# Expert stage of a mixture-of-experts layer: from row tiles of 128 with x stationary to units of up to 320 rows with the weights stationary

## The chip, the cores and the metric

One NeuronCore of one Trainium2 chip runs the whole program. The metric is the device time of one execution in microseconds (us). The engines are TensorE (PE in the rows; PEld is its weight load), VectorE (DVE), ScalarE (ACT), GpSimd (POOL) and SyncE (SP), which issues most DMAs. In rows, an SPq or POOLq is the queue of DMAs that the engine issues.

## What is computed

The reference is one encoder layer on 4096 tokens of 1024 numbers, all float32. First a Fourier mixer and a layer norm, then a mixture of experts and a second layer norm. The expert part, cut to its core:

```python
scores = sigmoid(xt @ w_router)                    # 4096 x 32
# best of 4 groups of 8 experts, then the top 2 experts in that group
gate = gate / gate.sum(-1, keepdims=True)
hb = silu(xb @ w_gate[e]) * (xb @ w_up[e])         # 1024 -> 512
y  = hb @ w_down[e]                                # 512 -> 1024
out = segment_sum(y * gate, token)
x = layer_norm(2 ** 0.25 * x + out, g, b)
```

Every token goes to 2 of 32 experts, 8192 rows in all. The reference's inputs send 243, 248, 228, 257, 289, 307, 203, 209, 278, 289, 220, 242, 258, 266, 246, 235, 249, 265, 273, 272, 298, 202, 199, 308, 251, 239, 206, 278, 281, 245, 257 and 351 rows to experts 0 to 31. Sixteen experts have more than 256 rows; only the last has more than 320. Tiles of 128 rows, at least two per expert, are then 80. Units of up to 320 rows are 33: 16 with more than 256 rows ("wide"), 17 with fewer ("narrow"), the second unit of the last expert among these, with 31 rows.

## The kernel before

The kernel has three parts: the Fourier mixer with router (its code is not touched, apart from the layout of the lists), the expert stage, and the final layer norm. Between the first two, the routing writes for each expert a list of (token, gate) pairs to HBM by scattered DMAs, and VectorE works out a table of tile numbers (`tstart`, lines 1260 to 1267) that all engines load into registers.

Matrix products keep float32 precision with three passes: each operand is split in a high part (a cast to float32r, on ScalarE) and a low part (the rest, a subtraction on VectorE), and `PASSES` takes high x high, high x low, low x high. So each weight goes through 12 pieces of 128x1024 per expert: DMA into a ring `wraw` of `SLOTS` (4) pieces, cast (line 981), subtraction (line 1246). Gate and up weights have two buffers (`wgu`, one per expert parity, 64 KiB per partition each); the down weights `wd` have one.

The expert stage runs `expert_tiles` on every engine: a loop over pairs of experts; each expert has two tiles written out and a loop over further tiles under an `If`. A tile on TensorE (`tile`, from line 864) is: gate, 24 matmuls of 512 columns (line 859), with the x rows stationary and the weights moving; up, 48 matmuls of 256 columns in two halves; two transposes of `hid`, four of the next tile's x, and again two and four (lines 852 and 845), the x rows coming from a gather by token number; down, 24 matmuls of 512 columns (line 889), two banks `psY`. ScalarE does silu (999), the high parts of `hidT` (1004) and x (990), weight casts, and half of the gated output (1012). VectorE does the product (1289), the low parts (1295, 1276), weight subtractions, and the other half of the output (1303). The weight pieces of the next expert are spread over the first two tiles by hand (`EARLY`, `LATE`).

GpSimd moves the rows: an indirect gather of 128 rows into `xrow` (1448) and an indirect scatter that adds `yrow` to `sums` in HBM (1456), each scatter waited for before the row numbers are replaced (1459 to 1461). SyncE loads weight pieces in order (`load_piece`), each when its slot has been freed by VectorE's subtraction, and the lists, one DMA for each expert (550).

Of the kernel before, what the change touches and what calls it, by code (L numbers as in the profile page):

```python
# [15 lines left out]
P = 128  # L16
# [4 lines left out]
CH = D // P  # L21
# [30 lines left out]
def shape_constants():  # L52
# [36 lines left out]
    for t in range(TILES):  # L89
        for m in range(P):  # L90
# [5 lines left out]
    ebase = (np.arange(E) * RANKS)[None, :] * np.ones((P, 1))  # L96
    steps = (np.arange(S // P) * P)[None, :] * np.ones((P, 1))
    parts = [("f1", f1), ("ident", np.eye(P)), ("before", before), ("ones", np.ones((P, P))),
             ("cs", cs), ("alt", alt), ("first", first), ("firstg", firstg),
             ("ebase", ebase), ("steps", steps)]  # L100
# [78 lines left out]
def trunk_kernel(nc, x, w_in, w_out, router_w, router_b, w_gate, w_up, w_down, ln_g, ln_b,  # L179
# [5 lines left out]
    lists = nc.dram_tensor("expert_lists", [P * E * BLOCKS, 2], I32).ap()  # L185
# [3 lines left out]
    with ExitStack() as ctx:  # L189
# [17 lines left out]
        def sem(name):  # L207
# [24 lines left out]
        cmp = at("cmp", 176, D)[0:1, :].rearrange("p (e j) -> p e j", e=E)  # L232
# [3 lines left out]
        wgu = [[at(f"wgu{b}_{n}", kib, 2 * CH * F, F32R).rearrange("p (m c f) -> p m c f", m=2, c=CH)  # L236
                for n, kib in (("hi", lo), ("lo", lo + 32))] for b, lo in enumerate((0, 128))]
        wd = [at(f"wd_{n}", kib, FC * D, F32R).rearrange("p (c f) -> p c f", c=FC)
              for n, kib in (("hi", 64), ("lo", 80))]
        mxT = [at(f"mxT_{n}", kib, D, F32R).rearrange("p (c n) -> p c n", c=CH)  # L240
               for n, kib in (("hi", 96), ("lo", 100))]
        hidT = [at(f"hidT_{n}", kib, F, F32R).rearrange("p (c n) -> p c n", c=FC)
                for n, kib in (("hi", 104), ("lo", 106))]
        xrow = at("xrow", 108, D)
        wraw = at("wraw", 112, SLOTS * D).rearrange("p (s d) -> p s d", s=SLOTS)
        yrow, sgate, hid = at("yrow", 192, D), at("sgate", 196, F), at("hid", 198, F)
# [8 lines left out]
        tstart = keep.take("tstart", E + 1, I32)  # L255
        desti = keep.take("desti", 4, I32)
        payg = keep.take("payg", 8, I32)
        entry_t = keep.take("entries", 2 * 2 * BLOCKS, I32)
        rowg = keep.take("rowg", 4, I32)
        ixg = keep.take("ixg", 1, I32)  # L260
        sx = keep.take("sx", 1, I32)
        sxn = keep.take("sxn", 1, I32)
        eps_c, eps2_c = keep.take("eps_c", 1), keep.take("eps2_c", 1)
        zer = keep.take("zer", E)
        rb = keep.take("rb", E)
        mid = keep.take("mid", CH * NG)
        padl = keep.take("padl", 2 * BLOCKS, I32)
# [28 lines left out]
        first, firstg, ebase, steps = (cview(n) for n in ("first", "firstg", "ebase", "steps"))  # L296
# [4 lines left out]
        entries = entry_t.rearrange("p (b r w) -> p b r w", b=2, w=2)  # L301
# [19 lines left out]
        xrow_s = xrow.rearrange("p (d c) -> p c d", c=CH)  # L321
# [37 lines left out]
        tab_ok = sem("tab_ok")  # L359
        ab_ps, ab_hi, ab_lo, xl_ev = sem("ab_ps"), sem("ab_hi"), sem("ab_lo"), sem("xl_ev")  # L360
        wraw_in = [sem(f"wraw_in{n}") for n in range(SLOTS)]
        whi_ok, wlo_ok = sem("whi_ok"), sem("wlo_ok")
        entries_in = [sem("entries_in0"), sem("entries_in1")]
        xrow_in, y_out, ixg_ok, sx_ok = sem("xrow_in"), sem("y_out"), sem("ixg_ok"), sem("sx_ok")
        g_ps, ua_ps, ub_ps, x0_ps, x1_ps, xh_ev, xlo_ev = (
            sem(n) for n in ("g_ps", "ua_ps", "ub_ps", "x0_ps", "x1_ps", "xh_ev", "xlo_ev"))
        silu_ok, hida_ok, hidb_ok, h0_ps, h1_ps, hh_ev, hl_ev = (
            sem(n) for n in ("silu_ok", "hida_ok", "hidb_ok", "h0_ps", "h1_ps", "hh_ev", "hl_ev"))
        y0_ps, y1_ps, ya_ok, yd_ok = (sem(n) for n in ("y0_ps", "y1_ps", "ya_ok", "yd_ok"))
# [56 lines left out]
        def gu_piece(b, part, j):  # L426

            w = wgu[b][part][:, j // 4]
            return w[:, 2 * (j % 4):2 * (j % 4) + 2, :].rearrange("p c f -> p (c f)")

        def block_of(t, lo):

            return (t - lo).with_bounds(min_val=0, max_val=BLOCKS - 1) if t is not lo else 0

        def gate_of(t, b, lo):

            return entries[:, b, ds(block_of(t, lo), 1), 1].bitcast(F32)

        EARLY, LATE = ((), (4, 5)), ((0, 1, 2, 3), (6, 7))

        def entries_there(eng, e, b, kind):
            if kind == 0:
                eng.wait_ge(entries_in[b], 8 * e + 16 - 8 * b)

        def expert_tiles(eng, tile):


            def expert(i, b, last=False):  # L450
                lo = eng.value_load(tstart[0:1, ds(2 * i + b, 1)], min_val=0, max_val=MAX_TILES)
                hi = eng.value_load(tstart[0:1, ds(2 * i + b + 1, 1)], min_val=2, max_val=MAX_TILES)
                tile(lo, 2 * i + b, b, lo, 0, last)
                tile(lo + 1, 2 * i + b, b, lo, 1, last)
                with eng.If(hi > lo + 2):
                    with eng.Fori(lo + 2, hi) as t:
                        tile(t, 2 * i + b, b, lo, 2, last)

            with eng.Fori(0, E // 2 - 1) as i:
                for b in range(2):  # L460
                    expert(i, b)
            expert(E // 2 - 1, 0)
            expert(E // 2 - 1, 1, last=True)
# [1062 lines left out]
```

## Times and profile before

| | |
|---|---|
| runs | 2432.01, 2433.85, 2435.06 us; median 2433.85 |
| profiled execution, span | 2431.3 us (its own time is not given beside it) |
| TensorE busy | 2224.0 us (91%), 12032 matmuls |
| VectorE, ScalarE, GpSimd busy | 1337.8, 909.3, 606.1 us |
| data moved | 438.13 MB, mean 180 GB/s |
| first gate matmul of the expert stage | 847.54 us |
| last down matmuls of the expert stage | 2293.58 us |

The busy time of an engine is a sum over stages. The expert stage is about 1450 us of the span, so its windows are read apart from the rest. The granted clock is a share of 2.4 GHz: 1.00 is 2.4 GHz, 0.50 is 1.2 GHz. Matmuls are pipelined, so their durations overlap; the time from one start to the next is what they cost.

### The profile page before, as it was taken

Reading aid. Unit: us, or ns where it says so; the run is one execution under the profiler, and the core shown is the slowest. Engines: PE = TensorE matmul, PEld = TensorE weight load, DVE = VectorE, ACT = ScalarE, POOL = GpSimd, SP = SyncE. Lnnn points to the kernel's source line nnn. Section 1 sums busy time; section 2 is a strip of 40 time slices with the busy share of each in tenths; the row PEclk is TensorE's granted clock in tenths of the full one; section 3 lists DMA queues with packets and bytes.
Section 4 is the critical chain, followed back from the end, with each engine's and each line's share of the span. In section 5 each row is a group of like instructions: output and inputs, shape, how many; then the busy total and the mean of one; then the engine's idle time right before and its main releaser. Section 6 shows DMA issues by size and latency. Waiting matters only on the chain.

```text
span 2431.3 us, 36221 instructions
## 1 busy us (share of the span) xinstructions
PE 2224.0 (91%) x12032; PEld 1827.0 (75%) x12033; DVE 1337.8 (55%) x2246; ACT 909.3 (37%) x1335; POOL 606.1 (25%) x672
## 2 busy tenths in 40 slices
PE   8999899999998299999999999999999999999700
PEld 3443778878886288888898898888888988988600
DVE  3221348888878555444544544554445455444298
ACT  2221123223333245434534534534345345443143
POOL 1000035454444412111211111111212111111166
PEclk9999999999999599999999999999999999999955
DMA  5980233333433377665765765865667678656386
GB/s 217 289 281 0 80 143 128 126 127 119 142 123 122 124 232 235 182 183 172 241 184 170 245 180 169 241 198 164 178 177 236 189 223 245 181 173 174 78 297 239
DMA packets 128121, 438.13 MB, mean 180 GB/s; under 512 B 24624, under 2 KB 26672, under 8 KB 123952
## 3 DMA queue, kind: packets, MB, share of 16 engines
q1 hardware_dynamic: 88736, 301.72, 35.5%
q0 software_dynamic: 39344, 135.88, 22.5%
q8 instruction: 24, 0.39, 0.1%
q14 instruction: 17, 0.14, 0.0%
HBM read 326.33 MB, written 112.26 MB: 180 GB/s over the span
## 4 chain that ended last, share of the span: by engine, by line
PE 91%; POOL 3%; issue 3%; DVE 2%; DMA 1%; ACT 0%; SPq 0%; POOLq 0%; DVEq 0%
PE ps L859 37%; PE ps L889 18%; PE ps L746 15%; PE ps L683 5%; PE ps L845 3%; POOL fin_r L1489 3%; PE ps L728 2%; PE ps L702 2%; PE ps L780 2%; PE ps L852 2%; PE ps L637 1%; PE ps L767 1%; PE ps L687 1%; PE ps L646 1%; PE ps L742 0%
## 5 line engine op out<-in xcount | busy, mean ns | idle before, releaser
L1246 DVE TENSOR_TENSOR wgu_lo<-wraw,wgu_hi 128x1024 fp32r<-128x1024 f32 x256 | 299.6, 1221 | 176.0 <-ACT wgu_hi L981 156.5
L859 PE MATMUL ps<-wgu_hi,mxT_hi 128*128 128x256 f32 (+1 forms) x1920 | 338.9, 319 | 1.6 <-DVE mxT_lo L1276 1.6
L859 PE MATMUL ps<-wgu_lo,mxT_hi 128*128 128x256 f32 (+1 forms) x1920 | 337.8, 318 | 0.0
L859 PE MATMUL ps<-wgu_hi,mxT_lo 128*128 128x256 f32 (+1 forms) x1920 | 337.8, 318 | 0.0
L859 PEld LDWEIGHTS ps<-wgu_hi,mxT_hi 128*128 128x128 f32 x1920 | 290.9, 191 | 33.7 <-issue 2.4
L859 PEld LDWEIGHTS ps<-wgu_lo,mxT_hi 128*128 128x128 f32 x1920 | 285.3, 191 | 25.0
L859 PEld LDWEIGHTS ps<-wgu_hi,mxT_lo 128*128 128x128 f32 x1920 | 285.3, 191 | 24.9
L981 ACT CAST wgu_hi<-wraw 128x1024 fp32r<-128x1024 f32 x256 | 253.6, 1062 | 20.3 <-DMA wraw<-expert_w_up 20.3
L1289 DVE TENSOR_TENSOR hid<-sgate,ps 128x256 f32<-128x256 f32 x160 | 67.2, 420 | 337.0 <-PE ps L859 337.0
L1456 POOL DMA_INDIRECT sums<-yrow,sx x81 | 131.4, 1622 | 296.4 <-DVE yrow L1303 270.9
L1004 ACT CAST hidT_hi<-ps 128x256 fp32r<-128x256 f32 x160 | 59.6, 372 | 381.7 <-PE ps L852 381.7
L889 PE MATMUL ps<-wd_hi,hidT_hi 128*128 128x512 f32 x640 | 179.5, 402 | 0.0
L889 PE MATMUL ps<-wd_lo,hidT_hi 128*128 128x512 f32 x640 | 171.9, 390 | 0.0
L889 PE MATMUL ps<-wd_hi,hidT_lo 128*128 128x512 f32 x640 | 171.1, 389 | 0.0
L1246 DVE TENSOR_TENSOR wd_lo<-wraw,wd_hi 128x1024 fp32r<-128x1024 f32 x128 | 148.5, 1221 | 40.8 <-ACT wd_hi L981 40.8
L999 ACT ACTIVATE sgate<-ps 128x512 f32<-128x512 f32 x80 | 47.8, 598 | 312.9 <-PE ps L859 312.7
L981 ACT CAST wd_hi<-wraw 128x1024 fp32r<-128x1024 f32 x128 | 126.5, 1051 | 44.0 <-PE ps L889 31.9
L889 PEld LDWEIGHTS ps<-wd_lo,hidT_hi 128*128 128x128 f32 x640 | 120.2, 188 | 26.6
L889 PEld LDWEIGHTS ps<-wd_hi,hidT_lo 128*128 128x128 f32 x640 | 120.1, 188 | 25.2
L1460 POOL COPY sx<-sxn 128x1 int32<-128x1 int32 x81 | 15.1, 186 | 482.3 <-DMA sums<-yrow,sx 482.3
L928 ACT CAST xt_hi<-ps 128x256 fp32r<-128x256 f32 x128 | 40.4, 379 | 245.7 <-PE ps L728 243.9
L889 PEld LDWEIGHTS ps<-wd_hi,hidT_hi 128*128 128x128 f32 x640 | 114.4, 189 | 19.5
(175 smaller groups left out, 3373.3 us busy)
## 6 DMA issues: line engine op xcount, KB each, us to landing
wraw<-expert_w_gate SPq DMA_DIRECT2D x128, 512.0 KB, 6.5
wraw<-expert_w_up SPq DMA_DIRECT2D x128, 512.0 KB, 4.2
wraw<-expert_w_down SPq DMA_DIRECT2D x128, 512.0 KB, 4.4
xch<-x SPq DMA_DIRECT2D x16, 1024.0 KB, 8.8
first_stage<-ych SPq DMA_DIRECT2D x16, 1024.0 KB, 9.6
yt<-first_stage SPq DMA_DIRECT2D x16, 1024.0 KB
fin_r<-sums SPq DMA_DIRECT2D x32, 512.0 KB, 4.0
out<-fin_r SPq DMA_DIRECT2D x32, 512.0 KB, 2.9
```

Source lines behind the costliest of these rows:

```text
L683: mm = nc.tensor.matmul(dst, foldT[:, m, g, c * P:(c + 1) * P], T[:, m, g, h * HALF:(h + 1) * HALF], start=(g == 0), stop=(m == 1 and g == ...
L702: nc.tensor.matmul(bank[s1_bank(n)], f1, xch[:, b, n % 4 // 2, n % 2 * HALF:(n % 2 + 1) * HALF], start=True, stop=True).then_inc(job_ps, 1)
L746: mm = nc.tensor.matmul(ps[:, cols], xt[l][:, m, c, :], w[r][:, c, cols], start=(n == 0 and c == 0 and not edge_row), stop=(n == 2 and c = ...
L845: mm = nc.tensor.transpose(psX0[:, c * P:(c + 1) * P] if half == 0 else psX1[:, c * P:(c + 1) * P], xrow_s[:, 4 * half + c, :], ident)
L859: mm = nc.tensor.matmul(ps, mxT[l][:, c, :], wgu[b][r][:, m, c, lo:hi], start=(n == 0 and c == 0), stop=(n == 2 and c == CH - 1))
L889: mm = nc.tensor.matmul(psY[:, cols], hidT[l][:, c, :], wd[r][:, c, cols], start=(n == 0 and c == 0), stop=(n == 2 and c == FC - 1))
L981: nc.scalar.copy(dst, wraw[:, j % SLOTS, :]).then_inc(whi_ok, 1)
L1004: nc.scalar.copy(hidT[0][:, 2 * half:2 * half + 2, :].rearrange("p c n -> p (c n)"), psH[half]).then_inc(hh_ev, 1)
L1246: nc.vector.tensor_tensor(lo, wraw[:, j % SLOTS, :], hi.bitcast(F32), ALU.subtract).then_inc(wlo_ok, 1)
L1289: nc.vector.tensor_tensor(hid[:, cols], sgate[:, cols], psU[half], ALU.mult).then_inc(ok, 1)
L1456: pool.indirect_dma_start(acc, bass.IndirectOffsetOnAxis(ap=sx[:, 0:1], axis=0), yrow, None, compute_op=ALU.add).then_inc(y_out, 16)
L1489: nc.gpsimd.tensor_tensor(fin_r[:, b, :], fin_r[:, b, :], lnb2, ALU.add).then_inc(fh_ok, 1)
```

## The change

The expert stage is written anew. In words:

- **Units.** The stage is one loop over units of one expert and up to 320 rows. A unit is three row blocks: two of 128 (`t` = 0, 1) and one of 64, which only wide units use. The table holds for each unit its expert, its row in the list, whether it is wide, and a running count of wide units. VectorE makes it with unit numbers on 128 partitions, TensorE turns it into a row with three matmuls (`psTab`), VectorE takes it to `utab`.
- **Stationary weights.** Gate and up go over four blocks `k` of 128 hidden columns; the weight block is stationary, x (transposed, all rows of the unit, 256 or 320 columns) moves. The result comes out with hidden features on the partitions, so `hid` needs no transposes. `If` and `Else` hold the two widths.
- **Down.** For the two blocks of 128 rows as before, with `hidT` stationary. For the 64 rows of a wide unit, `hidC` holds the high part of the 64 rows in its first 64 columns and the low part in the other 64; 8 matmuls per half with both parts of the weights give all four products, of which the two halves of the partitions are added on ScalarE (`ycross`) and VectorE (`y_c`).
- **Buffers.** One buffer each for gate, up and down weights. `wraw` has 6 slots. x rows, output rows and list entries are held for three blocks.
- **Order.** While the up product runs, the gate weights of the next unit are split; up weights follow during down; the down weights of a unit are split at its own start. GpSimd in unit u: gather for u + 1, two or three scatters, each waited for, then the copy of the row numbers.
- **Lists.** 64 lanes instead of 128; a unit's entries are loaded by four small DMAs.

What the engines do after the up product, in the order of their programs (`split j` is weight piece j of the next unit: 0 to 3 gate, 4 to 7 up):

- TensorE: x turns 0 and 1, down of block 0 half 0, x turn 2, half 1, x turn 3, block 1 half 0, the 64 rows' turn (`turn_xc`, if the next unit is wide), half 1, and for a wide unit `down_c` for both halves.
- ScalarE: x turns 0 and 1, `hidC`, split 4, `y_half` 0, x turn 2, split 5, x turn 3, `y_half` 1, the 64 rows' turn, splits 6 and 7, and `y_cross` twice if wide.
- VectorE: x turns 0 and 1, `hidC`, split 3, x turn 2, split 4, `y_half` 0, split 5, x turn 3, the 64 rows' turn, split 6, `y_half` 1, split 7, and `y_c` twice if wide. Before, in its first part: splits 8 to 11 of the unit itself, then splits 0 to 2 of the next, each ahead of one block's product and low part.

The core of the diff:

```diff
-        wgu = [[at(f"wgu{b}_{n}", kib, 2 * CH * F, F32R).rearrange("p (m c f) -> p m c f", m=2, c=CH)
-                for n, kib in (("hi", lo), ("lo", lo + 32))] for b, lo in enumerate((0, 128))]
+        wu = [chunks(f"wu_{n}", kib, CH) for n, kib in (("hi", 0), ("lo", 16))]
+        wg = [chunks(f"wg_{n}", kib, CH) for n, kib in (("hi", 64), ("lo", 80))]
...
@@ SyncE @@
+            with sp.Fori(1, units) as u:
+                e, row = unit_expert(sp, u), unit_row(sp, u)
                 for j in range(PIECES):
+                    load_piece(u, e, j)
+                    if j == 1:
+
+                        own_wait(sp, ent_ok, u, sp_gate)
+                        load_entries(row)
...
@@ TensorE @@
-            def up_or_gate(ps, b, m, lo, hi):
-                for n, (l, r) in enumerate(PASSES):
-                    for c in range(CH):
-                        mm = nc.tensor.matmul(ps, mxT[l][:, c, :],
-                                              wgu[b][r][:, m, c, lo:hi],
-                                              start=(n == 0 and c == 0), stop=(n == 2 and c == CH - 1))
-                return mm
...
+            def gate_or_up(ps, w, k, n):
+                for i, (l, r) in enumerate(PASSES):
+                    for c in range(CH):
+                        mm = nc.tensor.matmul(ps[k % 2][:, 0:n], w[l][:, c, k * P:(k + 1) * P],
+                                              mxT[r][:, c, 0:n], start=(i == c == 0),
+                                              stop=(i == 2 and c == CH - 1))
+                return mm
+
+            def first_products(u, n):
+                pe.wait_ge(wlo_ok, PIECES * u + 4)
+                for k in range(FC):
+                    if k >= 2:
+                        pe.wait_ge(silu_ok, 4 * u + k - 1)
+                    gate_or_up(psG, wg, k, n).then_inc(g_ps, 1)
+                pe.wait_ge(wlo_ok, PIECES * u + GU_PIECES)
+                for k in range(FC):
+                    if k >= 2:
+                        pe.wait_ge(hid_ok, 4 * u + k - 1)
+                    gate_or_up(psU, wu, k, n).then_inc(u_ps, 1)
...
+            def down_c(u, h):
+                cols = slice(h * HALF, (h + 1) * HALF)
+                for r in range(2):
+                    for c in range(FC):
+                        mm = nc.tensor.matmul(psY[h], hidC[:, c, :], wd[r][:, c, cols],
+                                              start=(r == c == 0), stop=(r == 1 and c == FC - 1))
+                mm.then_inc(yc_ps, 1)
+
+            def unit(u, more):
+                wide = unit_wide(pe, u)
+                pe.wait_ge(xh_ev, 4 * u + 4)
+                pe.wait_ge(xlo_ev, 4 * u + 4)
+                pe.wait_ge(xch_ev, u + 1)
+                pe.wait_ge(xclo_ev, u + 1)
+                with pe.If(wide > 0):
+                    first_products(u, UNIT)
+                with pe.Else():
+                    first_products(u, NARROW)
+                if more:
+                    pe.wait_ge(xrow_in, 32 * u + 64)
+                    turn_x(0)
+                    turn_x(1)
+                pe.wait_ge(wlo_ok, PIECES * u + PIECES)
+                pe.wait_ge(ya_ok, 2 * u + 2)
+                pe.wait_ge(yc_ok, 2 * u + 2)
+                down(u, 0, 0, y0_ps)
+                if more:
+                    pe.wait_ge(xlo_ev, 4 * u + 5)
+                    turn_x(2)
+                pe.wait_ge(yd_ok, 2 * u + 2)
+                down(u, 0, 1, y1_ps)
...
+                pe.wait_ge(ya_ok, 2 * u + 3)
+                down(u, 1, 0, y0_ps)
...
+                pe.wait_ge(yd_ok, 2 * u + 3)
+                down(u, 1, 1, y1_ps)
...
@@ ScalarE @@
+            def unit(u, more):
+                wide = unit_wide(act, u)
+                act.wait_ge(y1_ps, 2 * u + 2)
+                act.wait_ge(yc_ps, 2 * u + 2)
+                for k in range(FC):
+                    split(u, GU_PIECES + k)
+                    act.wait_ge(g_ps, 4 * u + k + 1)
+                    nc.scalar.activation(sgate[:, k, :], psG[k % 2][:, 0:UNIT], ACT.Silu).then_inc(silu_ok, 1)
+                for k in range(FC):
+                    if more:
+                        split(u + 1, k)
+                    act.wait_ge(hid_ok, 4 * u + k + 1)
+                    nc.scalar.copy(hidT[:, 0, k, :], hid[:, k % 2, :]).then_inc(hh_ev, 1)
...
@@ GpSimd @@
+                if more:
+                    pool.wait_ge(x_ps, 4 * u + 4)
+                    pool.wait_ge(xc_ps, u + 1)
+                    gather(u + 1)
+                    gather_c(u + 1)
+                    nc.gpsimd.tensor_copy(ent_next, ent_in).then_inc(ent_ok, 1)
+                for t in range(2):
+                    pool.wait_ge(ya_ok, 2 * u + t + 3)
+                    own_wait(pool, yd_ok, 2 * u + t + 3, pool_gate)
+                    scatter(t, P, y_out)
+                    own_wait(pool, y_out, 32 * u + 16 * t + 16, pool_gate)
```

## Rows read from the trace of the kernel before

**Rows 1.** The page's chain that ended last: by engine, by line.

```profile
PE 91%; POOL 3%; issue 3%; DVE 2%; DMA 1%; ACT 0%; SPq 0%; POOLq 0%; DVEq 0%
PE ps L859 37%; PE ps L889 18%; PE ps L746 15%; PE ps L683 5%; PE ps L845 3%; POOL fin_r L1489 3%; PE ps L728 2%; PE ps L702 2%; PE ps L780 2%; PE ps L852 2%; PE ps L637 1%; PE ps L767 1%; PE ps L687 1%; PE ps L646 1%; PE ps L742 0%
```

**Rows 2.** Windows, the expert stage: length, busy (instructions) by engine, clock, DMA, GB/s.

```profile
844.00:2295.00 1451.00, 1449.03 (x8648) 1291.76 (x8648) 732.21 (x938) 639.24 (x889) 267.46 (x400) 1.00 0.66 193
```

**Rows 3.** Timeline of TensorE, first gate matmuls of tiles 1, 3, 4 and 79.

```profile
867.28 1.98 PE L859 MATMUL ps<-wgu_hi,mxT_hi 128*128 128x512 f32 x8
...
903.40 1.98 PE L859 MATMUL ps<-wgu_hi,mxT_hi 128*128 128x512 f32 x8
...
921.58 2.11 PE L859 MATMUL ps<-wgu_hi,mxT_hi 128*128 128x512 f32 x8
...
2276.42 1.98 PE L859 MATMUL ps<-wgu_hi,mxT_hi 128*128 128x512 f32 x8
```

**Rows 4.** Timeline of TensorE over one tile: start, us, what.

```profile
2131.90 1.98 PE L859 MATMUL ps<-wgu_hi,mxT_hi 128*128 128x512 f32 x8
...
2137.34 1.11 PE L859 MATMUL ps<-wgu_hi,mxT_hi 128*128 128x256 f32 x8
...
2143.10 0.38 PE L852 MATMUL ps<-cst,hid 128*128 128x128 f32 x2
...
2144.41 1.17 PE L889 MATMUL ps<-wd_hi,hidT_hi 128*128 128x512 f32 x4
2145.42 1.08 PE L889 MATMUL ps<-wd_lo,hidT_hi 128*128 128x512 f32 x4
...
2149.96 1.98 PE L859 MATMUL ps<-wgu_hi,mxT_hi 128*128 128x512 f32 x8
```

**Rows 5.** Groups by line and form, 900 to 2200 us: busy, mean ns, idle before.

```profile
L1246 DVE TENSOR_TENSOR wgu_lo<-wraw,wgu_hi 128x1024 fp32r<-128x1024 f32 x232 | 271.4, 1221 | 162.1 <-ACT wgu_hi L981 143.2 <-issue 10.6
L981 ACT CAST wgu_hi<-wraw 128x1024 fp32r<-128x1024 f32 x232 | 229.8, 1062 | 0.0
...
L1276 DVE TENSOR_TENSOR mxT_lo<-ps,mxT_hi 128x512 fp32r<-128x512 f32 x144 | 92.8, 686 | 4.7
...
L1289 DVE TENSOR_TENSOR hid<-sgate,ps 128x256 f32<-128x256 f32 x144 | 60.5, 420 | 290.9 <-PE ps L859 290.9
...
L999 ACT ACTIVATE sgate<-ps 128x512 f32<-128x512 f32 x72 | 43.0, 598 | 276.7 <-PE ps L859 276.5
```

**Rows 6.** Timeline of all engines after the last tile.

```profile
2293.58 1.07 PE L889 MATMUL ps<-wd_hi,hidT_lo 128*128 128x512 f32 x4
2294.93 0.75 DVE L1303 TENSOR_SCALAR yrow<-ps,entries 128x512 f32<-128x512 f32 x1 [3.98 <-PE ps L889]
2296.48 1.58 POOL L1481 DMA_INDIRECT sums<-yrow,sx  x1 [11.49 <-DVE yrow L1303]
2302.58 0.82 SPq L592 DMA_DIRECT2D fin_r<-sums  x2
```

**Rows 7.** Timeline of ScalarE at the start of an expert pair.

```profile
927.17 1.28 ACT L999 ACT_TABLE_LOAD   x1
928.46 0.60 ACT L999 ACTIVATE sgate<-ps 128x512 f32<-128x512 f32 x1
```

**Rows 8.** The scatter's line 1456, 81 of them: issue to landing.

```profile
DMA to landing us min/median/max: 5.9/7.5/10.3
```

**Rows 9.** A gather of 128 rows of 4 KiB, line 1370, 32 of them: issue to landing.

```profile
DMA to landing us min/median/max: 4.2/5.1/5.8
```

**Rows 10.** Timeline of all engines ahead of the first tile.

```profile
822.33 1.21 DVE L1260 TENSOR_TENSOR cmp<-base,cst 1x1024 f32<-1x1024 f32 x1
...
836.47 1.01 POOL L1448 DMA_INDIRECT xrow<-h_rows,ixg  x1 [0.92 <-POOL ixg L1467]
...
843.98 1.94 PE L845 MATMUL ps<-cst,xrow 128*128 128x128 f32 x8 [25.96 <-DMA xrow<-h_rows,ixg]
...
847.54 3.62 PE L859 MATMUL ps<-wgu_hi,mxT_hi 128*128 128x512 f32 x8 [1.61 <-DVE mxT_lo L1276]
```

More of the change, by code:

```diff
@@ L443, in entries_there, with piece @@
[L443 to L463, printed above, removed]
+        def piece(part, j):
+            if j < GU_PIECES:
+                w = (wg, wu)[j // 4][part]
+                return w[:, 2 * (j % 4):2 * (j % 4) + 2, :].rearrange("p c f -> p (c f)")
+            return wd[part][:, j - GU_PIECES, :]
@@ L831, in _ @@
             ranks(GROUPS - 1)
-            pe.sem_inc(x1_ps, 1)
-            pe.sem_inc(y1_ps, 1)
+            pe.wait_ge(utab_made, 1)
+            for k in range(3):
+                mm = nc.tensor.matmul(psTab[:, k * P:(k + 1) * P], ucol[:, k:k + 1], ident,
+                                      start=True, stop=True)
+            mm.then_inc(utab_ps, 1)
+            pe.sem_inc(y1_ps, 2)
+            pe.sem_inc(yc_ps, 2)
             pe.wait_ge(p_ev, GROUPS)
@@ new lines, in down @@
+            def down(u, t, h, done):
+                cols = slice(h * HALF, (h + 1) * HALF)
+                for i, (l, r) in enumerate(PASSES):
+                    for c in range(FC):
+                        if t == h == 0 and i != 1:
+                            pe.wait_ge(hh_ev if i == 0 else hl_ev, 4 * u + c + 1)
+                        mm = nc.tensor.matmul(psY[h], hidT[:, l, c, t * P:(t + 1) * P], wd[r][:, c, cols],
+                                              start=(i == c == 0), stop=(i == 2 and c == FC - 1))
+                mm.then_inc(done, 1)
@@ L901, in _ @@
+            pe.wait_ge(xrow_in, 32)
+            turn_x(0)
+            turn_x(1)
+            for k in (2, 3):
+                pe.wait_ge(xlo_ev, k - 1)
+                turn_x(k)
+            pe.wait_ge(xlo_ev, 3)
+            wide0 = unit_wide(pe, 0)
+            with pe.If(wide0 > 0):
+                pe.wait_ge(xcrow_in, 16)
+                turn_xc()
+            with pe.Else():
+                pe.sem_inc(xc_ps, 1)
+            all_units(pe, unit)
         @block.scalar
@@ L1311, in invert @@
+            for j in range(2, GU_PIECES):
+                split(0, j)
+            for k in range(4):
+                turn_x(0, k)
+            take_xc(0)
+            dve.sem_inc(yd_ok, 2)
+            dve.sem_inc(yc_ok, 2)
+            all_units(dve, unit)
             def invert(t, b):
```

566 lines of the change are left out of this document (318 added, 248 removed).

## Prediction

> **What bounds the kernel now.** I read the chain of waits first. It is TensorE for 91% of the span, and line 859 (gate and up) with line 889 (down) are over half of it [rows 1]. So the first question is whether TensorE ever waits in the expert stage. The row of that stretch says no: 1449.03 us busy in 1451.00, at full clock, DMA engines at 0.66 [rows 2]. Next the period. The first gate matmuls of the second tile and of the last one start at 867.28 and 2276.42, 78 tiles apart, so one tile takes 18.066 us; between them lie all loop ends, register loads and skipped third tiles, and the only visible excess is about 0.1 us in one period (903.40 to 921.58) [rows 3]. The stage is therefore a pure count of TensorE instructions. The other engines matter only if their order makes TensorE wait.
>
> **Prices on TensorE** [rows 4]. 24 gate matmuls of 512 columns take 2131.90 to 2137.34, 226.7 ns each. 48 up matmuls of 256 columns take 2137.34 to 2143.10, 120.0 ns each. The difference is 0.417 ns a column, which is one column per cycle of 2.4 GHz, plus 13 ns whatever the width. Twelve transposes take 1.31 us, 109 ns each. Down: 20 matmuls from 2145.42 to 2149.96, 227 ns each, after about 0.1 us of waiting at its start. Together 5.44 + 5.76 + 1.31 + 5.55 = 18.06.
>
> **The change on TensorE.** Before, 80 tiles: 80 x 18.066 = 1445.3 us. After, 33 units, 16 wide and 17 narrow (the counts stand with the reference; the unit of 31 rows is run as 256).
>
> - Narrow unit: gate and up are 2 x 4 x 24 = 192 matmuls of 256 columns, 23.0 us. Down is 48 of 512, 10.9. Sixteen transposes of x, 1.75. With 0.1 of lag, 35.8 us, against 36.1 for the two tiles it replaces. The hidden transposes go, but gate now pays the fixed 13 ns twice as often.
> - Wide unit: 192 matmuls of 320 columns. The trace has no such width. Below it is bounded by the 256-column price (120 ns), above by the 512-column price (227 ns). Two widths and one per-column price make a line, so I take 120.0 + 64 x 0.417 = 146.7 ns, 28.2 us. Down is 48 + 16 = 64 matmuls, 14.5 us. The 64-row transposes I price like full ones, 24 x 0.109 = 2.6. Sum 45.4 us, against 54.2 for three tiles.
> - Stage: 17 x 35.8 + 16 x 45.4 = 1335.0 us, that is 110.3 less. All of the gain is in the wide units, 16 x 8.8 = 141, plus 5 from the narrow ones, less one additional unit (35.8) for the last expert.
>
> If 320 columns cost what 256 do, 82 us more are saved; if what 512 do, 246 more are spent. The common slope speaks against both; I keep 2 ns either way (6 us).
>
> **Do the others keep up?** Prices [rows 5]: a weight cast 1.06 us on ScalarE, its subtraction 1.22 on VectorE, silu 0.60 and the x subtraction 0.69 for 512 columns, the hidden product 0.42 for 256, and the gated output 0.75 [rows 6]; a 512-column cast out of the banks I take like silu. Scaled by columns, ScalarE has about 21 us a unit and VectorE 23 to 25, in 35.8 or 45.4. Totals fit; what counts is order. Let U be the end of the last up matmul and T the end of the unit (U + 12.8 narrow, U + 17.2 wide).
>
> - After U: product 0.49, high part about 0.43, so the last hidden chunk is ready at U + 1.1. TensorE does eight transposes and three matmuls first, until U + 1.6. Covered.
> - Output banks: down of tile 1 needs the two halves of tile 0 taken by U + 7.3 and U + 10.0. ScalarE: last high part to U + 1.2, two x turns to 2.4, the copy for the 64 rows to 2.8, a weight cast to 3.9, its half 0.69, U + 4.6. VectorE: last low part to 1.7, two x turns to 3.2, its copy to 3.6, a weight to 4.8, the third x turn (ScalarE's part ends at 5.2) to 5.9, a weight to 7.1, its half 0.75, U + 7.9. Covered.
> - Single weight buffers: the last up pieces of the next unit are subtracted by about T + 2.5, wanted at T + 11.5. The down pieces are done by T + 13, wanted after T + 24. Double buffering gave slack that nothing used.
> - Silu of the first gate group must be done before the third group begins, at T + 5.8 (narrow). ScalarE comes free at about T + 0.8 and then has a table load, one cast, a second table load and silu, if the unit loop is given both loads as the pair loop is: T + 0.8 + 1.3 + 1.06 + 1.3 + 0.43 = T + 4.9. The margin is 0.9 us, the thinnest here. It rests on a table load costing 1.28 us and no more: the trace shows load at 927.17 and silu at 928.46 [rows 7]. The Trainium skill (ScalarE: Activation LUTs, What ACT_TABLE_LOAD costs) adds some 1.4 us of drain to each switch of set, 2.66 us in all; by that, silu would end at T + 7.6 and 32 units would wait 1.8 us each, 58 us in sum. The trace disagrees, so the sum above stands.
> - GpSimd is serial: scatter, wait, scatter, wait, then the next gather. A scatter lands in 7.5 us in the median, 10.3 at most [rows 8]; a gather by row numbers in 5.1 [rows 9]. GpSimd starts 0.8 us after the output is written (2295.68 to 2296.48, [rows 6]), so scatter 0 starts at U + 8.7, which is T - 4.1 (narrow) or T - 8.6 (wide). Two scatters of 7.6 to 7.9 with their issue bring the narrow unit to T + 11.5; the wide one has a third and is at T + 14.7. Copies, waits and two gather issues take some 3.6, the landing 5: the next rows are there at T + 20 and T + 23.4. TensorE wants it at the next U: T + 23 or T + 28. Covered, except wide followed by narrow (7 times), where it just about meets. I add nothing.
> - Branches: TensorE now takes four per unit. The pair loop now jumps over six tile bodies for about 0.1 us at most [rows 3]. I take 0; the other end, 4 x 0.1 x 33, is 13 us.
> - DMA: 33 instead of 32 sets of weights in 8% less time, so 0.66 becomes about 0.73 [rows 2]. A narrow unit asks as much per us as a two-tile expert does now, and that runs without a stall.
>
> **Head and tail.** The last routing group ends on VectorE where the unit table's arithmetic begins, 822.33 [rows 10]. The new table has some 16 small steps and three matmuls, about 9 us with the two weight splits now ahead of it; it ends before the first rows can arrive, since the gather goes at 836.47, its rows reach TensorE at 843.98 and gate starts at 847.54 [rows 10]. After: four entry loads instead of one, two gathers, and six weight pieces in the same queue instead of four. I take rows 3 us later; then four turns in two banks instead of two, 2 us, and 1.5 us for the second issue: 6.5 us later in all (3 to 12). At the end TensorE's last matmul is at 2293.58 to 2294.65 and the final load goes out at 2302.58 [rows 6]. Scatter 0 of the last unit lands about 2 us after TensorE ends and holds the second one: 1 us more.
>
> **Sum.** 2431.3 - 110.3 + 6.5 + 1.0 = 2328.5 us of span. The median of the runs is 2.5 us above that span, so 2331, 4.2% less.
>
> **Rivals.**
>
> 1. *Small stalls at unit boundaries.* The silu margin of 0.9 us gives way: with two more table loads in a unit (2.6 us, [rows 7]) by 1.7 us, with a slower loop end by some 0.5; 17 to 56 us in 33 units: 2348 to 2387. For: several slacks under 1 us, worked out from single rows. Against: TensorE has no such stall in 80 tiles. Chance 0.2.
> 2. *Branches run dry.* An If whose narrow arm lies 384 instructions on, and a loop end, meet at each unit's start. If a jump costs 1 to 2 us more than the queued matmuls cover, 33 to 66 us: 2364 to 2397. The rows show 0.1 us for the far jump back. The Trainium skill (Runtime: NRT & Kernel Launch, Instruction fetch mechanics) says that a taken branch out of the two fetched pages stops the engine for a fetch, which speaks against this change; the trace shows no such stop on TensorE, perhaps because 24 long matmuls are queued before it. Chance 0.08.
> 3. *GpSimd becomes the bound: slower or no gain.* If each scatter takes the longest landing of before, 10.3 us, wide units deliver at T + 31.5 and narrow ones at T + 25.5. That is 8.5 us late 7 times (wide, then narrow), 3.5 us 9 times (two wide) and 2.5 us 9 times (two narrow): 114 us, which eats the gain: 2445. It decides from 10 us a scatter; at 9 us it costs about 50. For: scatters now follow each other at once, and compete with weights. Against: the median of 7.5. Chance of slower 0.07.
> 4. *The change does not do what it says:* 320 columns cost more than the line. From 183 ns on, 36 ns over it, the gain is gone (3072 x 0.036 = 110). Chance 0.03, within which 0.02 ends within 0.2% or faster.
>
> **Numbers.** Forecast, no stall beyond a few us: 2318 to 2345, chance 0.58. Rivals 1 and 2: 0.28, both faster. Rival 3: 0.07. Rival 4: 0.03. Faster than 2318 (a shorter head, cheaper 64-row turns): 0.04. The range 2318 to 2385 leaves out that 0.04, the slow ends of 1 and 2 (about 0.06) and 3 and 4. A run tells 0.2%, about 5 us, from no change. Faster 0.90, the same 0.02, slower 0.08.
>
> **What would show it.** 192 gate and up matmuls between two groups of down, starting 120 ns apart (narrow) or 147 (wide). First gate to next first gate 35.8 and 45.4 us. First gate near 854, last matmul near 2189. Silu idle before TensorE, not TensorE before silu; no TensorE wait on the gathered rows. It is wrong if TensorE's chain shows waits on silu, on the rows, or on "issue" at unit starts.

## The result: no gain, TensorE waits for gathered rows

The changed kernel takes 2441.74 us in the median of 20 runs (2429.44 to 2452.31), the kernel before 2435.23 (2432.01 to 2439.32). The ratio is 1.0028, 95% interval [1.0015, 1.004]: slightly slower, where 2331 was forecast. The runs now spread over 23 us instead of 7, and the profiled one is among the fastest: span 2429.4, 101 us above the 2328.5 that the sum gave.

The page of the changed kernel, the chain that ended last, by engine and by line (before: [rows 1]):

```profile
PE 67%; DMA 19%; issue 6%; POOL 4%; DVE 2%; POOLq 1%; ACT 0%; SPq 0%; ACTq 0%; DVEq 0%
PE ps L867 19%; PE ps L749 15%; PE ps L891 12%; DMA sums<-yrow_b,ent_now 6%; DMA sums<-yrow_a,ent_now 6%; DMA xrow_b<-h_rows,ent_in 5%; PE ps L686 5%; POOL fin_r L1655 3%; PE ps L855 3%; DMA sums<-yrow_c,ent_now 3%; PE ps L731 2%; PE ps L705 2%; PE ps L783 2%; PE ps L640 1%; PE ps L899 1%
```

TensorE had 91% of the chain; now it has 67%, and scatters (into `sums`) and gathers (from `h_rows`) have 19%. The expert stage in one window, busy time in the order TensorE, its weight load, VectorE, ScalarE, GpSimd (before: [rows 2]):

```profile
860.00:2290.00 1430.00, 1369.72 (x8812) 1278.87 (x8813) 761.37 (x925) 722.92 (x989) 242.63 (x223) 0.98 0.70 192
```

The engine that was idle for 2 us in 1451 is idle for 60 in 1430. No other engine is near full, and the DMA engines are busy 0.70 of the time. So this looks like no shortage of throughput; something arrives late. TensorE's timeline at the first gate matmuls of unit 5 (320 rows) and unit 10 (256 rows), and the middle of unit 10:

```profile
1068.96 1.33 PE L867 MATMUL ps<-mxT_hi,wg_hi 128*128 128x320 f32 x8
1070.13 1.33 PE L867 MATMUL ps<-mxT_lo,wg_hi 128*128 128x320 f32 x8
...
1291.29 1.21 PE L867 MATMUL ps<-mxT_hi,wg_hi 128*128 128x256 f32 x8
...
1313.82 0.76 PE L867 MATMUL ps<-mxT_hi,wu_lo 128*128 128x256 f32 x5
1320.19 0.48 PE L855 MATMUL ps<-cst,xrow_a 128*128 128x128 f32 x1 [5.61 <-DMA xrow_b<-h_rows,ent_in]
...
1321.82 2.05 PE L891 MATMUL ps<-wd_hi,hidT 128*128 128x512 f32 x4
1323.67 1.91 PE L891 MATMUL ps<-wd_lo,hidT 128*128 128x512 f32 x4
```

Groups of eight 320-column matmuls start 1.17 us apart, 146.7 ns for each matmul, as forecast. Gate and up take 23.03 us in a narrow unit and 28.16 in a wide one (forecast 23.0 and 28.2). Then, between up and down, TensorE stands 5.61 us until the next unit's gathered rows are there, and when it starts again the four down matmuls take about twice the 0.9 us of a full clock. The windows say why (columns as in [rows 2]):

```profile
1310.00:1314.00 4.00, 4.00 (x36) 4.00 (x35) 2.61 (x4) 2.31 (x4) 2.32 (x2) 1.00 0.53 161
1314.00:1318.00 4.00, 0.58 (x5) 0.38 (x4) 0.98 (x2) 0.57 (x2) 0.53 (x1) 1.00 0.92 351
1318.00:1320.00 2.00, 0.00 (x0) 0.00 (x0) 0.00 (x0) 0.00 (x0) 0.00 (x0) 0.81 0.08 31
1320.00:1322.00 2.00, 1.80 (x9) 1.81 (x10) 0.03 (x1) 0.59 (x1) 0.19 (x1) 0.50 0.00 0
...
1324.00:1326.00 2.00, 2.00 (x6) 1.52 (x6) 0.85 (x1) 0.04 (x1) 0.00 (x0) 0.50 0.02 4
1326.00:1328.00 2.00, 2.00 (x12) 1.70 (x11) 0.00 (x0) 1.17 (x3) 0.00 (x0) 0.99 0.78 258
```

The granted clock falls from 1.00 to 0.50 (from 2.4 to 1.2 GHz) while TensorE stands and comes back at 1326. A long wait is paid a second time this way.

Over all 33 units I took from the same timeline the time from up's end to the first turn of x (the wait) and from there to the next gate (the rest). The stage is 95.8 us longer than 17 x 35.8 + 16 x 45.4, made of

- 59 us of waits for gathered rows. All narrow units but the first, the twelfth (number 11) and the last have one, of 2.1 to 5.8 us; of the wide ones only three (0.1, 0.7, 1.9);
- 25 us of slower clock. 21 of them stand behind waits: the rest is 1.4 to 2.8 us too long after each of the ten waits of 2.9 us and more, and 0.2 at most after the shorter ones. The other 4 are gate matmuls at half clock, 2.3 us in unit 0 (the clock is at 0.50 there from 860 to 864) and 1.4 in the last unit, behind 3.1 us of idling;
- 3.3 us once, where the loop is left for the last unit;
- 8 us of TensorE's own work, most of it at the 64-row turns of x and at down of the wide units.

The first gate is 6.2 us later than forecast, and the tail 1.65 us longer than before instead of 1. Against that, the sum took the old stage as 1445.3 us, where its first and last matmuls stand 1447.1 apart. 95.8 + 6.2 + 0.65 - 1.8 is the 101 us.

What GpSimd did around that wait, its timeline:

```profile
1283.59 1.68 POOL L1616 DMA_INDIRECT sums<-yrow_a,ent_now  x1 [9.43 <-DVE yrow_a L1410]
1292.76 1.59 POOL L1616 DMA_INDIRECT sums<-yrow_b,ent_now  x1 [7.49 <-issue]
1299.82 1.79 POOL L1616 DMA_INDIRECT sums<-yrow_c,ent_now  x1 [5.47 <-DMA sums<-yrow_b,ent_now]
1308.22 0.99 POOL L1638 COPY ent_now<-ent_next 128x6 int32<-128x6 int32 x1 [6.61 <-DMA sums<-yrow_c,ent_now]
1311.38 1.78 POOL L1602 DMA_INDIRECT xrow_a<-h_rows,ent_in  x1 [2.16 <-issue]
1313.46 1.07 POOL L1602 DMA_INDIRECT xrow_b<-h_rows,ent_in  x1 [0.30 <-issue]
1320.31 0.19 POOL L1626 COPY ent_next<-ent_in 128x6 int32<-128x6 int32 x1 [5.78 <-DMA xrow_b<-h_rows,ent_in]
```

Wide unit 9 ends at T = 1291.29. The forecast had the last scatter done at T + 14.7, the gather issued by T + 18.3 and the rows there at T + 23.4. It was T + 16.9, T + 22.2 and T + 28.9. Every part of the chain is some 1 to 2 us later than priced: the first scatter 0.9, the three together 1.3, from there to the second gather 1.6, the landing 1.6. No part is far off, but the sum had no margin.

### The profile page after: what moved, and what is told of

Read it like the earlier page. It is cut to its first block, busy times and chain, and to the rows that moved or that the text cites. A ratio compares the mean times of both kernels' runs of the same rounds, so it can differ in the third digit from the quotient of the medians.

```text
span 2429.4 us, 37501 instructions
## 1 busy us (share of the span) xinstructions
PE 2152.7 (89%) x12222; PEld 1819.1 (75%) x12223; DVE 1373.7 (57%) x2253; ACT 1000.2 (41%) x1442; POOL 580.5 (24%) x493
## 4 chain that ended last, share of the span: by engine, by line
PE 67%; DMA 19%; issue 6%; POOL 4%; DVE 2%; POOLq 1%; ACT 0%; SPq 0%; ACTq 0%; DVEq 0%
PE ps L867 19%; PE ps L749 15%; PE ps L891 12%; DMA sums<-yrow_b,ent_now 6%; DMA sums<-yrow_a,ent_now 6%; DMA xrow_b<-h_rows,ent_in 5%; PE ps L686 5%; POOL fin_r L1655 3%; PE ps L855 3%; DMA sums<-yrow_c,ent_now 3%; PE ps L731 2%; PE ps L705 2%; PE ps L783 2%; PE ps L640 1%; PE ps L899 1%
## 5 line engine op out<-in xcount | busy, mean ns | idle before, releaser
L891 PE MATMUL ps<-wd_hi,hidT 128*128 128x512 f32 x1056 | 302.1, 412 | 0.4 <-ACT hidT L1089 0.4
L891 PEld LDWEIGHTS ps<-wd_hi,hidT 128*128 128x128 f32 x1056 | 196.8, 195 | 38.3 <-ACT hidT L1089 0.8
L1349 DVE TENSOR_TENSOR wg_lo<-wraw,wg_hi 128x1024 fp32r<-128x1024 f32 x132 | 161.5, 1225 | 92.6 <-ACT wg_hi L1047 92.6
L1349 DVE TENSOR_TENSOR wu_lo<-wraw,wu_hi 128x1024 fp32r<-128x1024 f32 x132 | 160.7, 1218 | 52.3 <-ACT wu_hi L1047 52.2
L867 PE MATMUL ps<-mxT_hi,wg_hi 128*128 128x256 f32 (+1 forms) x1056 | 164.2, 298 | 12.7 <-issue 12.7
L867 PE MATMUL ps<-mxT_lo,wg_hi 128*128 128x256 f32 (+1 forms) x1056 | 163.1, 297 | 0.0
L867 PE MATMUL ps<-mxT_hi,wg_lo 128*128 128x256 f32 (+1 forms) x1056 | 162.5, 296 | 0.0
L867 PE MATMUL ps<-mxT_hi,wu_lo 128*128 128x256 f32 (+1 forms) x1056 | 161.9, 296 | 0.0
L867 PE MATMUL ps<-mxT_lo,wu_hi 128*128 128x256 f32 (+1 forms) x1056 | 161.8, 296 | 0.0
L867 PE MATMUL ps<-mxT_hi,wu_hi 128*128 128x256 f32 (+1 forms) x1056 | 161.8, 296 | 0.0
```

The source lines that it names most:

```text
L867: mm = nc.tensor.matmul(ps[k % 2][:, 0:n], w[l][:, c, k * P:(k + 1) * P], mxT[r][:, c, 0:n], start=(i == c == 0), stop=(i == 2 and c == CH ...
L891: mm = nc.tensor.matmul(psY[h], hidT[:, l, c, t * P:(t + 1) * P], wd[r][:, c, cols], start=(i == c == 0), stop=(i == 2 and c == FC - 1))
L1349: nc.vector.tensor_tensor(piece(1, j), wraw[:, j % SLOTS, :], piece(0, j).bitcast(F32), ALU.subtract).then_inc(wlo_ok, 1)
```

## The experiments

Each run is compared with runs of the kernel before on the same chip. The ratios are to the kernel before; the changed kernel's is 1.0028.

**The scatters out of the chain.** e1_no_scatter leaves out the three scatters of every unit and the waits for them; the experts' output is not added to the sums. e2_no_third_scatter leaves out only the 64-row one.

```diff
                 for t in range(2):
                     pool.wait_ge(ya_ok, 2 * u + t + 3)
                     own_wait(pool, yd_ok, 2 * u + t + 3, pool_gate)
-                    scatter(t, P, y_out)
-                    own_wait(pool, y_out, 32 * u + 16 * t + 16, pool_gate)
                 with pool.If(wide > 0):
                     own_wait(pool, yc_ok, 2 * u + 4, pool_gate)
-                    scatter(2, LANES, yc_out)
-                    own_wait(pool, yc_out, 16 * wides_to(pool, u), pool_gate)
```

> The changed kernel without its three scatters and their waits, so the experts' output is not added to the sums; all else as it is. Theory G (GpSimd's serial chain of scatters makes the next gather late): TensorE waits for rows no more, units take 35.8 to 37 us (narrow) and 44.6 to 45.9 (wide), no clock drop, stage about 1340 us after a first gate at 860; in all 2330 to 2340, some 100 less than the changed kernel. Rival W (the single weight buffers or the weight loads hold TensorE up): most of the stalls stay, 2400 to 2440, with TensorE waiting at gate or down instead of at the turn of the rows.

> The changed kernel without the scatter of the 64 rows of wide units, so their output is left out. Theory G: after a wide unit the next gather goes some 8 us earlier; the stalls of about 5 us in narrow units that follow a wide one, and their clock drops of 1.5 to 2.7 us, vanish (7 units, 45 to 50 us), the 2 to 3 us of narrow after narrow and the cascade behind it stay: 2385 to 2400. If the 64-row scatter is short and only a small part of the chain (as I had priced it, 3 us): 2420 to 2425.

e1_no_scatter: 2346.84 us, ratio 0.9638 [0.9622, 0.9654], 7 us above theory G's range and far from rival W's. No wait at the turn is left, and the stage exceeds its forecast by 13.3 us instead of 95.8 (2.2 of these are the first gate at half clock). e2_no_third_scatter: 2402.91 us, 0.9864 [0.9847, 0.988], 3 us above theory G's range. Every wait in a narrow unit behind a wide one is gone, while in narrow behind narrow eight of nine remain, 3.2 to 6.6 us, with falls of the clock. So the waits come with the scatters, and the third one accounts for less than half. That could be because GpSimd is held up, or because the scatters take DMA time from the gather; these two runs don't tell.

**The order on GpSimd, all work kept.** e4_gather_ahead keeps every transfer and moves the next unit's gather ahead of the wait for the last scatter and of the copy of the row numbers. Unit 0 is taken out of the loop for it.

```diff
             def unit(u, more):
-                wide = unit_wide(pool, u)
                 if more:
                     pool.wait_ge(x_ps, 4 * u + 4)
                     pool.wait_ge(xc_ps, u + 1)
                     gather(u + 1)
+                if not (isinstance(u, int) and u == 0):
+                    scatters_done(u - 1)
+                    own_wait(pool, ent_ok, u + 1, pool_gate)
+                    nc.gpsimd.tensor_copy(ent_now, ent_next).then_inc(entc_ok, 1)
+                    own_wait(pool, entc_ok, u + 1, pool_gate)
+                if more:
                     gather_c(u + 1)
...
-                if more:
-                    own_wait(pool, ent_ok, u + 2, pool_gate)
-                    nc.gpsimd.tensor_copy(ent_now, ent_next).then_inc(entc_ok, 1)
-                    own_wait(pool, entc_ok, u + 2, pool_gate)
```

> The changed kernel with GpSimd's program reordered: the next unit's gather is issued behind the last scatter, before the wait for it and before the row numbers are copied. Same work, same waits between scatters. Theory G: rows arrive 8 to 9 us earlier in every unit, all stalls at the turn vanish, 2335 to 2350. Rival Q (a gather queued behind a scatter of the same queue lands only after it): gather's landing grows from 6.5 to 12 us or more, rows come no earlier, 2400 to 2440.

2349.79 us, ratio 0.9648 [0.9632, 0.9664]: 92 us less than the changed kernel, with the same transfers. The same unit 10 in GpSimd's timeline (its up ends at 1291.2 here):

```profile
1277.17 1.43 POOL L1616 DMA_INDIRECT sums<-yrow_c,ent_now  x1 [5.69 <-DMA sums<-yrow_b,ent_now]
1278.90 1.67 POOL L1602 DMA_INDIRECT xrow_a<-h_rows,ent_in  x1 [0.30 <-issue]
1280.88 0.97 POOL L1602 DMA_INDIRECT xrow_b<-h_rows,ent_in  x1 [0.30 <-issue]
1285.17 0.89 POOL L1633 COPY ent_now<-ent_next 128x6 int32<-128x6 int32 x1 [3.33 <-DMA sums<-yrow_c,ent_now]
1290.18 0.40 POOL L1637 COPY ent_next<-ent_in 128x6 int32<-128x6 int32 x1 [4.12 <-DMA xrow_b<-h_rows,ent_in]
```

The gather is issued 1.7 us behind the third scatter instead of 11.6, and its rows are there before TensorE asks. Gathers now run beside a scatter and land later (median 7.8 us instead of 6.3), which eats little of that. Rival Q, by which the transfers would only wait for each other in the queue, falls. Behind narrow units the gather now waits for the list entries instead (82 us in 16 waits of GpSimd), which costs TensorE nothing here.

**How much slack there is.** e8_gpsimd_delay and e10_ahead_delay put the same idle work into both orders.

```diff
+                    for k in range(12):
+                        nc.gpsimd.tensor_copy(idle[:, k, :], ent_next)
                     nc.gpsimd.tensor_copy(ent_now, ent_next).then_inc(entc_ok, 1)
```

> The changed kernel with twelve additional small copies (of 6 numbers in each of 128 partitions, into a buffer that nobody reads; 0.19 us each, 2.3 us together) on GpSimd in each unit, behind the wait for the last scatter and ahead of the copy of the row numbers. Theory G (GpSimd's chain of scatters, waits and gather sets the period): nearly every one of the 32 turns moves by 2.3 us, with some further falls of TensorE's clock: 70 to 95 us more, 2510 to 2540. Rival D (the rows are late because the DMA engines are full of weights, whatever GpSimd does): under 2460.

> e4_gather_ahead with the same twelve copies (2.3 us) on GpSimd in each unit, again ahead of the copy of the row numbers, which now stands behind the issue of the next gather. Theory G (that order took GpSimd's chain off the path, with slack left): within 5 us of e4_gather_ahead, 2348 to 2355. Rival S (it is still at the edge): 20 to 70 us more, 2370 to 2420.

e10_ahead_delay: 2349.98 us, 0.9646 [0.9631, 0.9661], no difference from e4_gather_ahead; the new order has the slack. e8_gpsimd_delay: 2459.73 us, 1.0104 [1.0088, 1.0119], 18 us over the changed kernel. That is far under the 70 that theory G asked for at least, and 0.3 us under the rival's bound of 2460, which runs between 2447.86 and 2462.37 can't tell from it. Unit 10 shows it (timeline, GpSimd's rows and then TensorE's):

```profile
1308.51 2.17 POOL L1640 COPY idle<-ent_next 128x6 int32<-128x6 int32 x12 [6.16 <-DMA sums<-yrow_c,ent_now]
...
1314.27 0.98 POOL L1603 DMA_INDIRECT xrow_b<-h_rows,ent_in  x1 [0.30 <-issue]
1320.00 0.19 POOL L1627 COPY ent_next<-ent_in 128x6 int32<-128x6 int32 x1 [4.75 <-DMA xrow_b<-h_rows,ent_in]
...
1319.89 0.48 PE L856 MATMUL ps<-cst,xrow_a 128*128 128x128 f32 x1 [5.50 <-DMA xrow_b<-h_rows,ent_in]
```

The gather is issued 0.8 us later than in the changed kernel (1314.27 against 1313.46), yet its rows come 0.3 us earlier. Over the six narrow units behind a wide one it is issued 0.9 us later on average, and TensorE goes on 0.4 us later. So most of the additional 2.2 us of copies never reaches the gather's issue, and the moment of issue isn't all that sets its landing. From 1314 to 1318 the DMA engines are at 0.92 in the changed kernel; the down pieces of the weights were asked for just before:

```profile
1312.30 13.05 SPq L568 DMA_DIRECT2D wraw<-expert_w_down  x2
```

**The weights.** e9_light_weights loads a quarter of each piece. (A piece is 1024 columns wide, so 256 of 1024 are loaded, not the 128 of 512 that the expectation names.)

```diff
-                sp.dma_start(wraw[:, j % SLOTS:j % SLOTS + 1, :], w[:, ds(e, 1), h, :]
+                n = D if is_first(u) else D // 4
+                sp.dma_start(wraw[:, j % SLOTS:j % SLOTS + 1, 0:n], w[:, ds(e, 1), h, 0:n]
                              ).then_inc(wraw_in[j % SLOTS], 16)
```

> The changed kernel with a quarter of each weight piece loaded (128 of 512 columns) for all units but the first; the rest of the buffer keeps older numbers, so the output is not the reference's, and every instruction of the engines stays. It asks whether the scatters take 8 us because weights fill the DMA engines. Theory G (a scatter of 64 or 128 rows has this length of its own): scatter landing stays at 7 us or more in the median, TensorE still waits at the turn, 2415 to 2440. Rival D (contention): scatters land in 6 us or less, gathers in 4.5, each unit's chain is 5 to 8 us shorter, no waits at the turn: 2350 to 2375.

2349.79 us, ratio 0.9646 [0.9631, 0.9661]: rival D's number, with GpSimd's order unchanged, though scatters and gathers land 0.2 and 0.6 us later than rival D asked. Issue to landing of the scatters, changed kernel:

```profile
DMA to landing us min/median/max: 6.0/8.0/11.4
```

and with a quarter of the weights:

```profile
DMA to landing us min/median/max: 4.8/6.2/7.3
```

The gathers of 128 rows, changed kernel:

```profile
DMA to landing us min/median/max: 4.4/6.3/9.7
```

and with a quarter of the weights:

```profile
DMA to landing us min/median/max: 4.2/5.1/7.4
```

Two scatters and a gather are 1.8 + 1.8 + 1.2 = 4.8 us shorter, three scatters and a gather 6.6. The waits were 2.1 to 5.8. So contention is worth as much as the waits. To see whether that needs less traffic or only another moment, e11_up_held keeps every byte.

```diff
                 for j in range(PIECES):
+                    if j == 4:
+                        own_wait(sp, xrow_in, 32 * u + 32, sp_gate)
                     load_piece(u, e, j)
```

> The changed kernel with one additional wait in the DMA queue of the weights: the four up pieces of the next unit are asked for only when that unit's gathered rows have landed, instead of during the last two scatters and the gather. All bytes, all instructions and GpSimd's order stay. Theory B (the burst of weight pieces lengthens scatter b, scatter c and the gather by 1 to 2 us each, as the run with a quarter of the weights lets one think): scatter b and c and the gather land 1 to 2 us earlier, the waits at the turn shrink from 62 us to under 30, the clock falls less, 2365 to 2405. Rival V (what counts is the length of GpSimd's chain; the pieces then collide with scatter a instead, or come late for the up products): 2425 or more, or new waits of TensorE on the split of the up pieces.

2397.67 us, ratio 0.9847 [0.9827, 0.9867]: 44 us less than the changed kernel, inside theory B's range. The waits at the turn sum to 30 us, and gate and up take what they took, so the up pieces aren't late and rival V falls. Where the changed kernel had its up pieces at 1300.34 (the queue of the weights):

```profile
1300.34 9.20 SPq L568 DMA_DIRECT2D wraw<-expert_w_up  x4
```

this one has them behind the rows. Its weight queue in the same unit 10, which starts at 1283.79:

```profile
1289.01 3.03 SPq L568 DMA_DIRECT2D wraw<-expert_w_gate  x2
1307.93 1.82 SPq L568 DMA_DIRECT2D wraw<-expert_w_up  x4
```

GpSimd in it:

```profile
1293.98 1.43 POOL L1618 DMA_INDIRECT sums<-yrow_c,ent_now  x1 [7.09 <-DMA sums<-yrow_b,ent_now]
1299.09 0.19 POOL L1640 COPY ent_now<-ent_next 128x6 int32<-128x6 int32 x1 [3.68 <-DMA sums<-yrow_c,ent_now]
...
1302.86 1.07 POOL L1604 DMA_INDIRECT xrow_b<-h_rows,ent_in  x1 [0.30 <-issue]
1307.88 0.19 POOL L1628 COPY ent_next<-ent_in 128x6 int32<-128x6 int32 x1 [3.95 <-DMA xrow_b<-h_rows,ent_in]
```

And its windows:

```profile
1298.00:1302.00 4.00, 4.00 (x36) 4.00 (x35) 2.77 (x5) 1.41 (x2) 0.76 (x2) 1.00 0.03 5
1302.00:1306.00 4.00, 4.00 (x36) 4.00 (x35) 2.49 (x5) 2.22 (x4) 1.62 (x2) 1.00 0.60 181
```

The third scatter takes 5.1 us instead of 8.4 and the gather 5.0 instead of 6.9; the wait of this unit falls from 5.8 to 0.9 us. Over all wide units the third scatter's landing falls from 7.6 to 5.5 us in the median, while the first two keep theirs (8.1 and 8.2 before, 8.2 and 8.2 now). The step from the second scatter to the third is what it was (8.7 us in the median against 8.6). The DMA engines are still at 0.83 there (1290 to 1294), with gate pieces asked for at 1289.01, and about half of the waits stay.

**The branches.** e6_arms_swapped changes nothing but the order of the two arms on TensorE.

```diff
-                with pe.If(wide > 0):
-                    first_products(u, UNIT)
-                with pe.Else():
+                with pe.If(wide < 1):
                     first_products(u, NARROW)
+                with pe.Else():
+                    first_products(u, UNIT)
```

> The changed kernel with the two arms of TensorE's If exchanged, so that the narrow product, which the first unit takes, comes first. Theory B (the 9.5 us between the last turn and the first gate is TensorE's jump to the far arm, cold the first time): first gate at 853 to 856 instead of 860, 4 to 7 us less in all. Rival: the time is the entry of the loop itself or a register load; first gate stays at 860, no difference.

2431.77 us, ratio 0.9976 [0.9954, 0.9999]. The first gate in the changed kernel, behind the last turn of x:

```profile
850.32 0.42 PE L855 MATMUL ps<-cst,xrow_b 128*128 128x128 f32 x1
860.27 2.07 PE L867 MATMUL ps<-mxT_hi,wg_hi 128*128 128x256 f32 x8 [9.53 <-issue]
...
2254.90 2.07 PE L867 MATMUL ps<-mxT_hi,wg_hi 128*128 128x256 f32 x8 [3.14 <-issue]
```

and with the arms swapped:

```profile
851.61 0.28 PE L855 MATMUL ps<-cst,xrow_b 128*128 128x128 f32 x1
856.08 2.07 PE L867 MATMUL ps<-mxT_hi,wg_hi 128*128 128x256 f32 x8 [4.19 <-issue]
```

The first unit is narrow, and its arm lay behind 192 wide matmuls: that first jump costs 5.3 us (9.53 less 4.19). Inside the loop next to nothing changed: from a wide unit's turn to the next narrow gate it is 16.5 us in both, and gate and up of that narrow unit take 0.1 us less. But the 3.14 us of idling at 2254.90, at the copy of the unit behind the loop, are gone with the swap, and with them the 1.4 us of half clock behind them. The 4.19 us that are left ahead of the first gate stay unexplained.

**Both together.**

> The next gather issued ahead of the waits for the scatters (as in e4_gather_ahead), and the narrow arm of TensorE's branch first (as in e6_arms_swapped). Theory J (the first far jump of TensorE costs about 5 us in the head, and leaving the loop costs 3.3 us, both independent of the stalls): the two gains add, 2349.8 - 8 = 2341 to 2344, first gate 5 us earlier than in e4_gather_ahead (near 853), the last unit's rest 16.5 us instead of 19.7. Rival H (without the stalls the time goes back to the weight pieces or to the gathered rows): above 2347.

2342.24 us, ratio 0.9616 [0.9603, 0.9629]: the gains add (8 us expected, 7.6 measured), and rival H falls. The first gate is at 852.38. This is the best version, 94 us under the kernel before and 99 under the changed one.

## Why the prediction was wrong, step by step

- **TensorE's prices: right.** 120 and 146.7 ns for 256 and 320 columns; the units that wait for nothing take 35.85 us (35.8 forecast) and 45.85 (45.4). The 64-row turns, priced like full ones, cost 0.4 us a wide unit more.
- **The stage without waits: right.** In e7_ahead_and_arms the stage exceeds the forecast by 10 us, 2.8 of them in unit 0 (1.5 in the first gate at half clock, 1.3 ahead of the turn). Its span of 2337.5 stands beside the 2328.5 of the sum. The gain worked out for the change was there; it could not be had in this order.
- **The silu margin, single buffers, output banks: right.** TensorE's rows show no wait on silu, on a split or on a bank in the loop, and 0.4 us in all on a hidden chunk. The table loads take 1.28 us each and silu follows at once. Rival 1, which had 0.2, did not occur.
- **GpSimd, the step that failed.** "Covered, except wide followed by narrow (7 times), where it just about meets. I add nothing." The order of events was right and the third scatter rightly priced (8.0 us from its issue to the copy behind it, 7.8 forecast). Mis-sized was each step under load. From scatter to scatter it takes 9.1 and 8.6 us in the median instead of 7.6 to 7.9: the landing is 8.1 instead of 7.5, and 0.5 to 1.0 of overhead come on top instead of 0.1 to 0.4. The second gather lands in 6.7 instead of 5.1, a price read from gathers between 245 and 750 us, where the DMA engines were at 0.35. Behind a wide unit that makes up a wait of 5 us (6 times; the prediction's seventh place is ahead of the last unit, which waits for no next rows). For narrow behind narrow, where the margin was 3 us, unit 7 shows the same: its first scatter is at T - 4.0 as forecast, then come 9.3 (+ 1.5), 10.6 (+ 2.8), the copies (+ 0.2) and a gather of 8.4 (+ 3.3), and TensorE goes on at T + 28.0 instead of T + 23. Rival 3 named this mechanism. Its main price, 114 us at 10.3 us a scatter, is above the 80 of waits and the clock behind them. Its other, about 50 at 9 us a scatter, is near the 59 of waits, but by luck: its own terms give some 30 (a wide unit's rows at T + 27.5, 4.5 us late 7 times, and no other wait), since they had the gather at 5. It had a chance of 0.07, and the range left it out.
- **The clock: missing.** No term stood for what a wait costs behind its own end. It was 21 us behind the waits, a third on top of them.
- **Contention: seen and not used.** Rival 3 noted that scatters "compete with weights". DMA at 0.70 in the mean (0.73 forecast) hides bursts of 0.8 to 0.9, and these lay on the transfers that mattered: between issue and landing the share is 0.90 in the median for the first two scatters, 0.84 for the third, 0.89 for the second gather, their own bytes counted in.
- **Branches: right in the loop, wrong outside.** The loop pays 0.1 us at most, as [rows 3] let one expect; the first pass paid 5.3 us and the exit 3.3, with 1.4 of slower clock behind it. The Trainium skill (Runtime: NRT & Kernel Launch, Instruction fetch mechanics) says that a taken branch out of the pages held makes the engine wait for a fetch. The trace agrees at the first jump (5.3 us) and at the exit (3.3 us). In the steady loop it shows no such wait (0.1 us at most), and no run shows whether the targets there were out of the pages held.
- **The head.** Forecast 6.5 us, measured 12.7; 5.3 of the difference is that jump. **The tail** was 1.65 us longer instead of 1.

Three remedies were each nearly enough by themselves: no scatters (2346.8), a quarter of the weight bytes (2349.8), the gather earlier in the order (2349.8). They don't add, because a turn lacks at most 6 us and each gives about that or more. What is shown is that nearly all of the loss needs both, the chain and the contention. Why the delay in e8_gpsimd_delay cost 18 us instead of some 35 for the narrow units alone is only argued: the gather then falls into the end of the burst, and lands nearly as early as before. It was not tried to issue the scatters without waiting in between; the kernel waits because two of them may add to the same row.

## What to carry to other kernels

When the busiest engine is made faster, add up the whole serial chain of the engine that feeds it, from its first instruction to the landing of what is wanted, with the landing times of a loaded queue; where the slack comes out under a few microseconds, price the wait, and the clock behind it. An issue that has nothing to do with a wait ahead of it should be moved past that wait first: here this gave 92 us. A mean DMA share of 0.7 is no evidence that a transfer on the path runs undisturbed; look at the windows in which it runs.

## What was not expected of the hardware

- A scatter of 64 rows of 4 KiB takes nearly as long as one of 128 (7.6 against 8.1 us in the median from issue to landing). What shortens them is less traffic beside them: 5.1 and 6.3 us with a quarter of the weight bytes, and 5.5 for the 64 rows where the up pieces are held back.
- The granted clock fell to 0.50 in a wait of 5.6 us and stayed there for some 6 us of work. Ten waits of 2.9 us or more left 1.4 to 2.8 us behind them, waits of up to 2.5 us about 0.1. The length of a wait alone doesn't decide: one of 2.0 us in e8_gpsimd_delay (unit 7) left 1.7, with the clock at 0.56 to 0.58, and one of 3.0 us in e11_up_held (unit 22) left 0.1, with the clock at 1.00.
- A far jump of TensorE costs 5.3 us the first time and 0.1 us at most in the steady loop; the way out of the loop cost 3.3 us, and nothing when the narrow arm stood first.
